# mLSTM features and router by products of small matrices, up-projections by high and low parts

## The chip, the cores and the metric

The kernel runs on one core of one Trainium2 chip. The metric is the device time of one execution in microseconds: the median of three runs. Five engines work side by side, each in the order of its own list: TensorE (PE: products and transposes), VectorE (DVE), ScalarE (ACT), GpSimd (POOL) and SyncE (SP), which issues nearly all transfers. They wait for each other by semaphores that are counted up.

## The reference

Two blocks run one after the other on 256 tokens of width 1024. The first has two layers of three kinds of attention and an MLP with 4096 hidden features. The second, which the change is about, does this (cut to what matters; `c` is a context of 256 tokens, `l` the 256 tokens of the result):

```python
q_lat, kv_lat, k_rope, xm, z, g_mla, g_ml = split(modulate(rmsnorm(x_or_ctx)) @ w_in)  # 384,256,64,1024 x4
q = rmsnorm(q_lat, q_norm) @ w_uq             # 8 heads of 192, only for l
k, v = split(rmsnorm(kv_lat, kv_norm) @ w_ukv)  # 8 heads of 128 + 128, for c and l
y_mla = softmax(q k^T) v
x_c = silu(conv5(xm))                          # along the tokens, each feature by itself
q, k, v = blockdiag4(x_c, w_qblk), blockdiag4(x_c, w_kblk), blockdiag4(xm, w_vblk)
gates = concat(q, k, v) @ w_gate + b_gate      # 16 numbers a token: input and forget, 2 directions, 4 heads
h = mlstm forward + mlstm backward             # decays from running sums and running maxima of the gates
y_ml = sigmoid(z) * (rms(h) * ml_norm + ml_skip * x_c)
x = x + g1 * ((sigmoid(g_mla) * y_mla + sigmoid(g_ml) * y_ml) @ w_out)
hm = modulate(rmsnorm(x, norm2), shift2, scale2)
aff = softmax(hm @ w_router)                   # 16 experts, each takes its 32 best tokens
x = x + g2 * (sum over experts of aff * ((silu(xs @ w_gate_e) * (xs @ w_up_e)) @ w_down_e))
out = rmsnorm(x)
```

The experts' weights are 16 x 3 matrices of 1024 x 1024 in fp32, 201 MB of the 395 MB that the kernel moves.

## The kernel before

**Weights.** Every weight comes as a unit of at most 128 x 4 x 512 numbers (1 MB). SP issues the loads in one fixed order, and each waits (`slots_free`) for the unit whose slot it takes. In the first block and in the input projection of the second, four slots are in turn (`R1 = 4`). There a product is made of two parts: ACT writes the high part of a unit (`split2_hi`, L569) into `ring_hi`, POOL writes the rest over the unit itself (`split2_lo`, L575), and `split_product` (L1726) makes three products in the fast format fp32r instead of one in fp32. From unit `U8 = U_UQ` on the eight slots of the ring (ring_lo and ring_hi together) are used as they are, and `product` (L1719) multiplies in fp32, which the profile lists as two instructions a product. Four units hold `w_uq` (128 x 3 x 384), four `w_ukv` (128 x 2 x 512), four `w_out`. The experts follow with 192 units in 16 slots: the ring and eight in the arena (`more_slots`). The first four expert units take slots that `w_ukv` leaves, units 4 to 7 wait for the four of `w_out`, and 8 to 15 stand behind them in SP's list.

**Order of the second block**, as PE has it (`tensor_block2`, L651): the ten input tiles (`input_tile`, L674), in between the turning of `xm` into features (`xm_features`, L678); the up-projections (`banks`, L652); transposes of queries and keys; 18 rounds of attention over 16 pairs of head and token tile (L785), in which round j makes scores j, turns the weights j-1 and multiplies by values j-2; then the features of the mLSTM. These are made in full: queries and keys for all 512 tokens (L816), the skip path's transposes (L825), value features (L831), gates from all of them (L843), value tokens (`values`, L849), two products that pick out the gate rows (L861). DVE then makes 14 dependent steps of gate arithmetic on 8 partitions (`step`, L1202), with an Exp and a Ln of ACT between the third and the fourth. After all 14 PE turns the rows (L867), and the four heads follow (L899): decay rows, raw scores, numerators. Their norm, gain, gate and sum are one piece at the end (L1281 to L1295). The output projection (L931), the addition to x (`add_gated`, L1299), the norm (L1971), the transposes and the modulation follow, the router's 32 instructions (L939), the softmax, four rounds of the eight largest (L1338) with their indices, the spread of indices over the partitions (L952, L955), the matrices that pick tokens (L1350, L1352) and put them back (L1356), the gather of the first four experts (L976), and the experts (L959).

**Around it.** ACT's list (L1463 to L1484) has the high parts between the copies and sigmoids; at L1466 it waits for DVE's sums of squares of the latents and takes a root, then come the high parts 9 and 10 and only then the sigmoid of tile 3, which PE waits for (`sig_sb` 1, L707) before tile 4. POOL makes the block-diagonal matrices after the last unit of `w_ukv` (L1636).

## Time and profile before

| | us |
|---|---|
| median of 3 runs (1775.72 to 1781.25) | 1776.74 |
| profiled execution, its own time | 1783.21 |
| span of the profiled execution | 1781.4 |
| TensorE busy, share of the span | 1542.3, 87% |
| VectorE, ScalarE, GpSimd busy | 486.0, 501.8, 579.9 |
| mean granted TensorE clock, share of full speed | 0.928 |

The span goes from the first to the last instruction. Starts are counted from its beginning. A row of a timeline gives start, duration, engine, line, operation, what is written and read, the number of instructions merged into the row, and in brackets the idle time before it with what ended it. A matmul's duration holds its way through the array, so consecutive ones overlap; their pace is the distance of their starts.

### The profile page before, as it was taken

How to read it: one execution, taken by the hardware profiler on the slowest of the kernel's cores; microseconds unless marked ns; L12 is line 12 of the kernel's file. 1: busy time of each engine (PE TensorE's matmuls, PEld its weight loads, DVE VectorE, ACT ScalarE, POOL GpSimd, SP SyncE). 2: the span in 40 equal slices, each digit the busy share in tenths (PEclk: the TensorE clock that was granted, in tenths of full speed). 3: DMA queues.
4: the chain of work that ended last, by engine and by line, in shares of the span. 5: the costliest groups of instructions: out<-in, count | busy, mean ns of one | idle time of the engine just before them, and what ended most of it. 6: DMA issues, size and time to landing. Idle time of an engine off the chain costs nothing. (4 is left out here: it accounts for less than half of the span.)

```text
span 1781.4 us, 17171 instructions
## 1 busy us (share of the span) xinstructions
PE 1542.3 (87%) x7300; PEld 1007.1 (57%) x7300; DVE 486.0 (27%) x802; ACT 501.8 (28%) x654; POOL 579.9 (33%) x158
## 2 busy tenths in 40 slices
PE   6999999999999999999989999786876676676665
PEld 5776688877867678877878755464443131131111
DVE  1223332421222233232451348444220000000001
ACT  4255343333435344343433124322110000000000
POOL 4655277545746277744375310000000000000000
PEclk9999999999999999999999999978878787888887
DMA  6534455696444255598244630000649999999995
GB/s 239 170 117 140 142 175 180 225 335 220 165 142 135 102 189 178 176 356 285 92 148 142 218 123 1 1 14 1 240 190 421 422 422 421 421 421 422 421 421 247
DMA packets 124920, 395.37 MB, mean 222 GB/s; under 512 B 6679, under 2 KB 10580, under 8 KB 100268
## 3 DMA queue, kind: packets, MB, share of 16 engines
q1 hardware_dynamic: 122960, 388.66, 58.5%
q0 software_dynamic: 1456, 4.51, 0.7%
q8 instruction: 58, 0.95, 0.2%
q10 hardware_dynamic: 428, 1.10, 0.2%
q14 instruction: 18, 0.15, 0.0%
HBM read 393.19 MB, written 1.05 MB: 221 GB/s over the span
## 5 line engine op out<-in xcount | busy, mean ns | idle before, releaser
L585 POOL TENSOR_TENSOR ring_lo<-ring,ring_hi 128x2048 fp32r<-128x2048 f32 x101 | 467.6, 4633 | 364.3 <-ACT ring_hi L566 364.3
L1730 PE MATMUL psum<-ring_hi,hT_lo 128*128 128x512 f32 (+2 forms) x880 | 354.3, 403 | 17.3 <-DVE hT_lo L1994 10.2
L1732 PE MATMUL psum<-ring_hi,hT_hi 128*128 128x512 f32 (+2 forms) x880 | 344.7, 392 | 0.0
L1731 PE MATMUL psum<-ring_lo,hT_hi 128*128 128x512 f32 (+2 forms) x880 | 342.9, 390 | 0.0
L566 ACT ACTIVATE ring_hi<-ring 128x2048 fp32r<-128x2048 f32 x116 | 222.0, 1915 | 384.2 <-DMA ring<-in_w_in 121.3
L968 PE MATMUL psum<-arena 128*32 128x512 f32 x768 | 133.2, 858 | 97.1 <-DMA arena<-in_w_e_up 36.1
L1730 PEld LDWEIGHTS psum<-ring_hi,hT_lo 128*128 128x128 f32 x880 | 166.8, 190 | 59.0 <-issue 13.8
L1732 PEld LDWEIGHTS psum<-ring_hi,hT_hi 128*128 128x128 f32 x880 | 166.6, 189 | 36.8
L1731 PEld LDWEIGHTS psum<-ring_lo,hT_hi 128*128 128x128 f32 x880 | 167.4, 190 | 32.9 <-issue 0.5
L968 PE MATMUL psum<-ring,arena 128*32 128x512 f32 x768 | 137.4, 705 | 43.2 <-DMA ring<-in_w_e_gate 17.5
L968 PEld LDWEIGHTS psum<-arena 128*32 128x32 f32 x768 | 30.8, 150 | 199.7 <-issue 81.3
L1722 PE MATMUL psum<-ring,arena 128*128 128x512 f32 (+1 forms) x272 | 113.0, 574 | 0.8 <-ACT arena L2337 0.8
L968 PEld LDWEIGHTS psum<-ring,arena 128*32 128x32 f32 x768 | 31.6, 124 | 141.0 <-issue 65.3
L578 POOL TENSOR_TENSOR ring_lo<-ring,ring_hi 128x2048 fp32r<-128x2048 f32 (+2 forms) x20 | 87.5, 4383 | 61.7 <-ACT ring_hi L573 61.7
L1730 PE MATMUL psum<-ring_hi,uT_lo 128*128 128x512 f32 x256 | 101.5, 396 | 0.0
L1732 PE MATMUL psum<-ring_hi,uT_hi 128*128 128x512 f32 x256 | 100.6, 393 | 0.0
L1731 PE MATMUL psum<-ring_lo,uT_hi 128*128 128x512 f32 x256 | 99.8, 390 | 0.0
L1722 PEld LDWEIGHTS psum<-ring,arena 128*128 128x128 f32 x272 | 51.3, 190 | 58.1 <-issue 50.2
L1585 ACT ACTIVATE arena<-psum 128x512 f32<-128x512 f32 x8 | 4.3, 594 | 239.7 <-PE psum L968 239.7
L585 DVE TENSOR_TENSOR ring_lo<-ring,ring_hi 128x2048 fp32r<-128x2048 f32 x15 | 38.7, 2578 | 100.5 <-ACT ring_hi L566 100.5
L1730 PEld LDWEIGHTS psum<-ring_hi,uT_lo 128*128 128x128 f32 x256 | 48.1, 188 | 13.8 <-issue 4.2
L1732 PEld LDWEIGHTS psum<-ring_hi,uT_hi 128*128 128x128 f32 x256 | 48.1, 188 | 10.6
(342 smaller groups left out, 1549.8 us busy)
## 6 DMA issues: line engine op xcount, KB each, us to landing
ring<-in_w_in SPq DMA_DIRECT2D x60, 1024.0 KB, 5.0
ring<-in_w_up SPq DMA_DIRECT2D x32, 1024.0 KB, 5.8
ring<-in_w_down SPq DMA_DIRECT2D x32, 1024.0 KB, 5.9
ring<-in_w_e_gate SPq DMA_DIRECT2D x32, 1024.0 KB, 26.7
arena<-in_w_e_gate SPq DMA_DIRECT2D x32, 1024.0 KB, 26.4
ring<-in_w_e_up SPq DMA_DIRECT2D x32, 1024.0 KB, 26.7
arena<-in_w_e_up SPq DMA_DIRECT2D x32, 1024.0 KB, 26.7
ring<-in_w_e_down SPq DMA_DIRECT2D x32, 1024.0 KB, 27.3
```

The lines of the kernel that those rows point to most:

```text
L566: act.activation(slot_hi(u), slot(u), ACT.Copy).then_inc(hi_sb, 1)
L578: pool.tensor_tensor(slot_lo(u)[:, :, 0:n], slot(u)[:, :, 0:n], slot_hi(u)[:, :, 0:n].bitcast(F32), ALU.subtract)\
L585: eng.tensor_tensor(slot_lo(u), slot(u), slot_hi(u).bitcast(F32), ALU.subtract).then_inc(done, 1)
L968: mm = pe.matmul(psum[32 * j:32 * j + 32, bank + n, :], lhsT[:, 2 * q + c, 32 * j:32 * j + 32], both[:, c * D + n * UN:c * D + (n + 1) * U ...
L1585: act.activation(hid[:, n, :], psum[:, n, :], ACT.Silu).then_inc(hid_a, 1)
L1722: last = pe.matmul(dst, lhsT(k0 + k), slot(u)[:, first + k, 0:n], start=start and k == 0, stop=stop and k == nk - 1)
L1730: pe.matmul(dst, lo(k0 + k), w_hi, start=start and k == 0, stop=False)
L1731: pe.matmul(dst, hi(k0 + k), w_lo, start=False, stop=False)
L1732: last = pe.matmul(dst, hi(k0 + k), w_hi, start=False, stop=stop and k == nk - 1)
```

## The change

The diff does this, part by part.

1. The units of `w_uq` and `w_ukv` go through the four slots too, with high and low parts (`SPLIT2`, `U8 = U_OUT`), and the latents get high and low parts (`qlT_hi`, `qlT_lo`, `kvlT_hi`, `kvlT_lo`; five more instructions on DVE). The units of `w_out` are reordered: upper halves of the rows first.
2. In ACT's list the sigmoid of tile 3 and the high parts 9 to 11 stand ahead of the root of the latents; a small Sigmoid is put before them. DVE's later work waits for `lat_root` 2.
3. Six rounds of the attention (2, 4, ..., 12) get a piece each on PE and a copy on ACT: the block matrices are turned, and from them and `w_gate` are made a map from features to gates (`gates_map`) and a map from features to scores (`scores_map`).
4. After the attention queries, keys and value features are not made. The gates are 16 products of `xm` and `xc` with `gate_map`; the scores take `xc` and `pF`, eight products of `qk_map` with `xc` (`mapped`).
5. The gate steps are reordered, add_skip is put between them, PE turns `af` and `ab` after step 9 and starts decay rows after step 12.
6. In the heads: numerators wait for the half of the previous head that they overwrite; `zg` gets the gain in advance; norm, gate and sum of heads 0 to 2 (`head_out`) stand ahead of head 3's readout.
7. The output projection begins with the upper four feature chunks; the branch is added in pieces.
8. The router multiplies x itself, not the normed x, by a weight with the modulation in it, in 8 products over four column groups, and scales its 16 sums afterwards; a row for the shift comes from `router_bias`. The top rounds have no index step; a running count gives each chosen token its place, and `pick` is made by comparing the place with the slot number. Group 0 of the experts begins when half of its features of each engine are copied; `pickT` is turned out of `weighed` later.

```diff
-U8 = U_UQ = U_IN + 2 * len(IN_TILES)
+U_UQ = U_IN + 2 * len(IN_TILES)
 U_UKV, U_OUT, U_EX = U_UQ + 4, U_UQ + 8, U_UQ + 12
+U8 = U_OUT
+SPLIT2 = [(4, IN_TILES[i // 2][1]) for i in range(2 * len(IN_TILES))] + 4 * [(3, 384)] + 4 * [(2, UN)]
...
+            src += [chunks(wout[UN * kh:UN * kh + UN, UN * n:UN * n + UN]) for kh in range(2) for n in range(2)]
...
+                load_expert(U_EX + i, expert_unit(i), unit_done(U_OUT + (i >= R + 5) if R <= i < RE else U_EX + i - (R if i < R else RE)))
...
+            def banks(outs, hi, lo, u, n, kc):
+                unit_ready(u)
+                for b, t in outs:
+                    last = split_product(psum[:, b, 0:n], tokens(hi, t), lo(t), 0, u, nk=kc, n=n)
+                last.then_inc(slots_free, 1)
...
+            def turn_block(i):
+                pe.wait_ge(bd_sb, i + 1)
+                for c in range(KC):
+                    last = pe.transpose(flat[3][:, c * P:(c + 1) * P], bd[i][:, c, :], ident)
+                last.then_inc(map_full, 1)
+            def gates_map(i):
+                pe.wait_ge(rows_in, 32)
+                for c in range(KC):
+                    if i == 0:
+                        pe.matmul(psum[:, 6, c * 16:(c + 1) * 16], turned_bd[0][:, c, :], wg[:, c, :], start=True, stop=False)
+                    last = pe.matmul(psum[:, 6, c * 16:(c + 1) * 16], turned_bd[1][:, c, :], wg[:, (1 + i) * KC + c, :],
+                                     start=i == 1, stop=True)
+                last.then_inc(map_full, 1)
+            def scores_map():
+                for c in range(KC):
+                    last = pe.matmul(flat[3][:, c * P:(c + 1) * P], turned_bd[0][:, c, :], turned_bd[1][:, c, :], start=True, stop=True)
+                last.then_inc(map_full, 1)
             NJ2 = H2 * TT
...
+                if j in MAP_ROUNDS:
+                    i = MAP_ROUNDS.index(j)
+                    if i:
+                        pe.wait_ge(map_sb, i)
+                    if i < 2:
+                        turn_block(i)
+                    elif i == 2:
+                        gates_map(0)
+                    elif i == 3:
+                        scores_map()
+                    elif i == 4:
+                        turn_block(2)
+                    else:
+                        gates_map(1)
                 if j < NJ2:
...
+            values(1)
+            pe.wait_ge(map_sb, 6)
+            for i in range(4):
+                if i >= 2:
+                    pe.wait_ge(xc_sb, 2 * i - 2)
+                for j in range(4):
+                    c = 4 * (i % 2) + j
+                    feat = xm[:, c, :, 2:2 + T] if i < 2 else xc[:, c, :, :]
+                    last = pe.matmul(psum[32 * j:32 * j + 32, 6, :], gate_map[:, 1 - i // 2, c, :], feat, start=i == 0, stop=i == 3)
+            last.then_inc(gp_full, 1)
+            pe.wait_ge(y2_sb, NJ2)
+            mapped(0, 2)
+            pe.wait_ge(gp_sb, 1)
+            pe.matmul(psum[0:8, 7, :], const("sel_i"), gp, start=True, stop=True)
+            pe.matmul(psum[0:8, 6, :], const("sel_f"), gp, start=True, stop=True).then_inc(gr_full, 1)
+            pe.wait_ge(vt_sb, 1)
+            mapped(1, 0)
+            pe.wait_ge(skip_sb, 2)
+            pe.wait_ge(vt_sb, 2)
+            turn_skip(0, 1)
+            pe.wait_ge(p_sb, 1)
+            turn_skip(1, 2)
+            pe.wait_ge(p_sb, 2)
+            values(2)
+            pe.wait_ge(sk_v, 2)
+            values(3)
+            pe.wait_ge(gr_v, 9)
             for d in range(2):
                 for t in range(4):
-                    pe.transpose(psum[:, 4, 32 * d + 8 * t:32 * d + 8 * t + 8], (af, ab)[d][:, t * P:(t + 1) * P], ident[0:8, 0:8])
...
+            pe.wait_ge(gr_v, 12)
+            pe.wait_ge(vt_a, 2)
...
+                else:
+                    pe.wait_ge(dec_a, 10 * MH)
+                    spread(1, 0)
+                if h == 0:
+                    pe.wait_ge(at_sb, 3)
+                    pe.wait_ge(sk_v, 4)
+                for t in range(TT):
+                    if h:
+                        pe.wait_ge(h_v, 8 * h - 2 + 2 * t)
...
+            pe.wait_ge(mix_v, 10)
+            turn_gated(0, 0)
+            pe.wait_ge(gb_sb, 1)
+            pe.wait_ge(turn_a, TURN_A + 9)
+            out_unit(0, 0)
+            pe.wait_ge(mix_v, 16)
+            turn_gated(1, 3)
+            out_unit(1, 0)
...
+            def head_out(h0, h1, mv, ready):
+                heads = slice(TT * h0, TT * h1)
+                dve.wait_ge(hn_a, ready)
+                dve.tensor_scalar(hst[:, 1, heads], hst[:, 0, heads], 1.0 / MD, EPS, ALU.mult, ALU.add).then_inc(mix_v, 1)
+                dve.wait_ge(hn_a, ready + 1)
+                dve.reciprocal(hst[:, 3, heads], hst[:, 2, heads]).then_inc(mix_v, 1)
+                dve.wait_ge(mix_v, mv + 2)
+                dve.wait_ge(zg_sb, 4)
+                for h in range(h0, h1):
+                    for t in range(TT):
+                        v = h_tok[:, t, h * MD:(h + 1) * MD]
+                        dve.scalar_tensor_tensor(out=v, in0=v, scalar=hst[:, 3, 2 * h + t:2 * h + t + 1],
+                                                 in1=zg[:, t, h * MD:(h + 1) * MD], op0=ALU.mult, op1=ALU.mult).then_inc(mix_v, 1)
+                mv += 2 + TT * (h1 - h0)
+                cs = slice(MD * h0, MD * h1)
+                for t in range(TT):
+                    dve.wait_ge(mix_v, mv)
+                    dve.tensor_tensor(gated[:, t, cs], gated[:, t, cs], h_tok[:, t, cs], ALU.add).then_inc(mix_v, 1)
...
+            router_bias()
+            out_unit(0, 1)
+            out_unit(1, 1)
+            pe.wait_ge(rt_v, 1)
             for t in range(TT):
+                pe.wait_ge(x2_v, 4 + 2 * t)
                 for k in range(KC):
-                    last = pe.matmul(psum[:, 0, t * NE:(t + 1) * NE], hT[:, k, t * P:(t + 1) * P], wr[:, k, :],
-                                     start=k == 0, stop=k == KC - 1)
+                    last = pe.transpose(flat[(0, 3)[k // 4]][:, k % 4 * T + t * P:k % 4 * T + (t + 1) * P], eighths(x[:, t, :], k), ident)
+                    if t == 1 and k % 4 == 3:
...
+                    pe.wait_ge(turn_a, TURN_A + 10)
+                for j in range(4):
+                    k = 4 * half + j
+                    last = pe.matmul(psum[32 * j:32 * j + 32, 0, 0:T], wr[:, k, :], hT[:, k, :], start=half == 0, stop=half == 1)
...
+                                if g == 0 and part == 0 and c == 0 and n == 0 and j == 0:
+                                    pe.wait_ge((xs_v, xs_a)[q // 2], 2 + 2 * (q % 2))
...
+            def add_branch(n, ts, first):
+                cs = slice(n * UN, (n + 1) * UN)
+                g = g_row1[:, cs].unsqueeze(1).to_broadcast([P, TT, UN])
+                dve.tensor_tensor(x_tmp[:, ts, :], DB[1 + n][:, ts, :], g[:, ts, :], ALU.mult).then_inc(x2_v, 1)
+                dve.wait_ge(x2_v, first + 1)
+                dve.tensor_tensor(x[:, ts, cs], x[:, ts, cs], x_tmp[:, ts, :], ALU.add).then_inc(x2_v, 1)
+            dve.wait_ge(slots_free, unit_done(U_OUT + 2))
+            add_branch(0, slice(0, 2), 0)
+            dve.wait_ge(x2_v, 2)
+            dve.wait_ge(o2_half, 1)
+            add_branch(1, slice(0, 1), 2)
+            dve.wait_ge(slots_free, unit_done(U_OUT + 3))
+            add_branch(1, slice(1, 2), 4)
+            dve.wait_ge(turn_full, FULL + 7)
+            dve.tensor_copy(hT[:, 0:4, :], flat[0].rearrange("p (k t) -> p k t", k=4)).then_inc(turn_v, 1)
+            dve.wait_ge(norm_a, NORM_A + 4)
...
+            dve.tensor_copy(part_sums, psum[:, 0, 0:T]).then_inc(rt_v, 1)
+            dve.wait_ge(norm_v, NORM_V + 3)
+            dve.wait_ge(rt_v, 1)
+            dve.wait_ge(lg_full, 2)
+            for t in range(TT):
+                dve.scalar_tensor_tensor(out=aff[:, t, :], in0=psum[:, 1, t * NE:(t + 1) * NE], scalar=r_sq[:, t:t + 1], in1=router_row,
+                                         op0=ALU.mult, op1=ALU.add).then_inc(rt_v, 1)
+            dve.wait_ge(rt_v, 5)
+            dve.tensor_reduce(rst[:, 0, :], aff, AX_X, ALU.max, negate=True).then_inc(rt_v, 1)
...
+            for half in range(2):
+                for t in range(TT):
+                    act.wait_ge(x2_v, 2 if half == 0 else 4 + 2 * t)
+                    act.activation(xn[:, t, half * UN:(half + 1) * UN], x[:, t, half * UN:(half + 1) * UN], ACT.Square,
+                                   accum_out=sums2[:, t, half:half + 1]).then_inc(norm_a, 1)
+            act.wait_ge(turn_full, FULL + 8)
             act.activation(hT[:, 4:8, :], flat[3].rearrange("p (k t) -> p k t", k=4), ACT.Copy).then_inc(turn_a, 1)
-            act.wait_ge(x2_v, 4)
-            norm(x, xn)
-            act.wait_ge(mod_sb, 4)
-            turn_modulated(FULL + 8, hT, lambda k: amp2[:, k:k + 1], lambda k: shift2[:, k:k + 1])
-            act.wait_ge(rt_v, 1)
+            act.wait_ge(norm_v, NORM_V + 2)
+            act.activation(half_r, means2, ACT.Sqrt).then_inc(norm_a, 1)
...
+            top_step(dve.tensor_scalar(chosen, affT, 0.0, None, ALU.is_lt))
+            top_step(dve.tensor_tensor_scan(out=count, data0=chosen, data1=chosen, initial=0.0, op0=ALU.add, op1=ALU.max))
+            top_step(dve.tensor_tensor(place, chosen, count, ALU.mult))
...
+            act.activation(table_ahead, amp1[:, 0, 0:1], ACT.Sigmoid).then_inc(lat_root, 1)
+            sigmoid(3, zg[:, :, 0:UN], 2)
+            high_parts(9, 11)
             act.wait_ge(lat_sq, 6)
             act.activation(lat[:, 2, :], lat[:, 1, :], ACT.Sqrt).then_inc(lat_root, 1)
-            high_parts(9, 10)
-            sigmoid(3, zg[:, :, 0:UN], 2)
-            high_parts(11, 12)
+            high_parts(12, 12)
             xm_half(1)
...
-            high_parts(19, 19)
+            high_parts(19, 20)
             sigmoid(8, gated[:, :, 0:UN], 2)
+            high_parts(21, 22)
             sigmoid(9, gated[:, :, UN:D], 0)
+            high_parts(23, 27)
             for n in range(4):
...
```

## Rows read from the trace of the kernel before

**Rows 1.** Stretches: from:to, length, busy PE PEld DVE ACT POOL (instructions), clock, DMA share, GB/s.
```profile
1058.00:1113.30 55.30, 54.90 (x256) 30.08 (x256) 46.63 (x103) 21.56 (x49) 0.00 (x0) 1.00 0.00 1
1113.30:1170.60 57.30, 40.72 (x193) 22.80 (x193) 28.11 (x32) 17.50 (x20) 5.53 (x6) 0.86 0.03 10
...
1272.00:1316.70 44.70, 27.89 (x105) 23.38 (x104) 19.89 (x53) 7.87 (x18) 0.54 (x1) 0.62 0.55 224
1320.40:1763.40 443.00, 298.20 (x1627) 90.86 (x1616) 20.44 (x32) 14.44 (x26) 0.00 (x0) 0.83 1.00 417
```

**Rows 2.** The chain of waits around the output projection: start, us, what.
```profile
1242.14 29.91 PE psum L1722 x64
1272.07 1.23 DVE arena L1306
```

**Rows 3.** Timeline of SP's queue: loads of expert units.
```profile
1320.40 5.22 SPq L642 DMA_DIRECT2D ring<-in_w_e_up  x8
```

**Rows 4.** The timeline of ACT and PE at the latents' root.
```profile
917.98 0.21 ACT L1467 ACTIVATE consts<-consts 128x6 f32<-128x6 f32 x1 [8.38 <-DVE consts L1043]
...
921.80 1.28 ACT L1461 ACT_TABLE_LOAD   x1
923.10 1.02 ACT L1461 ACTIVATE arena<-psum 128x1024 f32<-128x1024 f32 x1
...
924.22 0.76 PE L1730 MATMUL psum<-ring_hi,hT_lo 128*128 128x512 f32 x1 [4.58 <-issue]
```

**Rows 5.** The timeline at a 384-column split product and in the up-projections.
```profile
906.22 0.34 PE L1730 MATMUL psum<-ring_hi,hT_lo 128*128 128x384 f32 x1
906.39 0.34 PE L1731 MATMUL psum<-ring_lo,hT_hi 128*128 128x384 f32 x1
...
889.93 3.52 POOL L578 TENSOR_TENSOR ring_lo<-ring,ring_hi 128x1536 fp32r<-128x1536 f32 x1 [13.88 <-ACT ring_hi L573]
...
1014.74 0.96 DVE L1099 COPY arena<-psum 128x768 f32<-128x768 f32 x1 [2.91 <-PE psum L1722]
...
1036.21 0.60 ACT L1489 ACTIVATE arena<-psum 128x512 f32<-128x512 f32 x1 [5.78 <-PE psum L1722]
...
1043.08 0.69 DVE L1105 COPY arena<-psum 128x512 f32<-128x512 f32 x1 [5.51 <-PE psum L1722]
```

**Rows 6.** The timeline of DVE beside POOL's last subtraction and after it.
```profile
992.41 4.60 DVE L1094 TENSOR_TENSOR arena<-xn 128x128 f32<-128x128 f32 x1
...
997.07 0.28 DVE L1094 TENSOR_TENSOR arena<-xn 128x128 f32<-128x128 f32 x1
```

**Rows 7.** The timeline of PE: transposes, gate products, router products.
```profile
1052.80 3.66 PE L779 MATMUL psum<-consts,arena 128*128 128x128 f32 x32
...
1138.38 5.34 PE L845 MATMUL psum<-arena 128*16 128x512 f32 x48 [1.21 <-ACT arena L1526]
...
1283.78 6.98 PE L941 MATMUL psum<-consts,hT 128*128 128x16 f32 x32 [2.13 <-issue]
```

**Rows 8.** The timeline of DVE and PE around the gate steps.
```profile
1153.59 0.68 DVE L1212 SCALAR_TENSOR_TENSOR xn<-xn 8x512 f32<-8x512 f32 x1 [2.71 <-ACT xn L1530]
...
1161.20 0.41 DVE L1228 TENSOR_TENSOR xn<-xn,hT 8x256 f32<-8x256 f32 x1
...
1170.61 2.04 PE L884 MATMUL psum<-hT,consts 8*128 8x256 f32 x4 [2.02 <-ACT consts L1536]
```

**Rows 9.** The timeline at the last head and its gain.
```profile
1217.34 6.30 PE L912 MATMUL psum<-arena 128*128 128x257 f32 x28 [2.91 <-DVE arena L1278]
...
1229.28 3.26 DVE L1290 SCALAR_TENSOR_TENSOR arena<-arena,consts 128x256 f32<-128x256 f32 x8
```

**Rows 10.** The timeline of DVE and PE before the experts.
```profile
1294.43 0.40 DVE L1342 MATCH_REPLACE8 consts<-consts 16x256 f32<-16x256 f32 x1
...
1277.97 3.68 PE L1769 MATMUL psum<-consts,xn 128*128 128x128 f32 x16 [5.94 <-DVE xn L1987]
...
1307.07 7.92 PE L979 MATMUL psum<-arena,xn 128*128 128x128 f32 x32 [0.84 <-DVE arena L1350]
```

494 lines of the change are left out of this document (237 added, 257 removed).

## The prediction

> **What bounds the kernel now.** I read the table of stretches first, then the chain of waits, then the timelines of each engine where the chain goes through it. While the experts run, the DMA share is 1.00 at 417 GB/s for 443 us [rows 1]: 176 units of 1.049 MB, 2.52 us each. Before it the DMA engines do almost nothing through the attention and the mLSTM (1 and 10 GB/s, [rows 1]), since the experts' slots hang on the output projection. So the kernel has two parts. The last one is bound by transfers and starts when the first expert units are used up: from SP's first issue of that kind at 1320.40 [rows 3] to the end of the span are 461.0 us, which nothing in the change touches. All before it is one chain of computation: PE in the attention (54.90 of 55.30 us busy), DVE, ACT and PE in turn in the features of the mLSTM (PE 40.72 of 57.30) and before the experts (27.89 of 44.70, clock 0.62) [rows 1]. Time saved there moves the last part forward one for one, as long as the transfers that can be issued early are done by then.
>
> **Part by part** (us, negative is saved). Each stage starts where PE ends the one before.
>
> *Order of ACT at the latents' root.* PE waits 4.58 before tile 4, until 924.22, for the sigmoid that ends at 924.12; that stood behind the root (917.98), two high parts and a table load [rows 4]. Tile 3 ends at about 917.7, so the sigmoid can end at 918.9 with its table loaded early, and PE goes on at about 919.7 after the transposes of `xm`. The row at 924.22 has 0.76 for a product that takes 0.39 at full clock: eleven starts lie 0.43 apart instead of 0.23, 2.2 lost after the wait. High part 9 ends at 920.8 and its subtraction (4.6) at 925.4, needed at 930.7 as tile 4 has four token tiles; the root comes at 926, and the copies after it are needed at 941. Sum: -4.5 - 2.2 = -6.7. If the clock falls anyway, -4.5; if a high part is late, 0.
>
> *Up-projections.* A unit of `w_uq` takes PE 0.96 + 2.91 = 3.87 now, one of `w_ukv` 1043.08 - 1036.21 = 6.87, which is 16 instructions of 0.43 [rows 5]. By parts a product of 384 columns starts every 0.17 [rows 5], one of 512 every 0.23: 18 x 0.173 = 3.1 and 24 x 0.229 = 5.5. Sum: 4 x (3.1 - 3.87) + 4 x (5.5 - 6.87) = -8.5. The splitting must hide: POOL takes 3.52 for 1536 numbers [rows 5], so 2.6 for 1152 and 2.3 for 1024; with ACT's 1.1 and a load of 4.0 (576 KB) one unit is ready 7.8 after its slot is free, and three units of PE last 9.3. For `w_ukv` it is 7.5 against 16. The tightest is the last unit of `w_uq`, with 1.3 to spare. If the load took 6.9 us, as those of `w_ukv` do when four are issued at once, up to four units would be late by 1.6 each: +6. Range -9 to -2.
>
> DVE has five more instructions and its two-input ones run beside POOL. The row shows 4.60 for 128 x 128 numbers beside a subtraction and 0.28 after it [rows 6]. The rotation of the queries (4.1) starts at about 1026, when POOL has just made its last part; PE needs the copies behind it 4 us later. I take 0, at most +4.
>
> By the Trainium skill (SBUF — State Buffer, on the shared port pair) a VectorE operation with two SBUF inputs and a GpSimd operation exclude each other for a whole instruction. The 4.60 agrees with that, as it is the length of POOL's subtraction. By that rule each of DVE's two-input operations between the new splits may wait up to 2.6, and the sum would be nearer to the +4.
>
> *Maps in the attention.* 24 transposes at 3.66/32 = 0.114 [rows 7] are 2.7; `gates_map` has 24 products of 16 columns, 48 instructions. With 6.98/32 = 0.218 at half clock [rows 7], 0.11 at full clock (PEclk is 1.00 in the attention): 5.3. `scores_map` is 16 instructions of 0.128: 2.1. PE is the bound there, so all of it counts: +10.1. ACT's copies (1.02, from 128 x 1024 as in [rows 4]) lie after an exp whose successors PE asks for in the next round, about 0.5 in time. If they come late in the four rounds: +3. The ends are +8 and +16.
>
> *From the attention to the first decay row.* Now 1170.61 - 1113.3 = 57.3 [rows 8]. After, counted from the attention's end: two `values` 4.1; gates 32 instructions at 5.34/48 = 0.111 [rows 7], 3.6, to 7.7 (the last Silu ends at 4.0, no wait); `mapped` 1.7 while DVE copies; two selections 1.7, to 11.3. DVE Ff and |Ff| to 12.8. ACT has a copy that waits for the second `mapped` (13.0), to 14.1, then table load, Exp, table load, Ln (1.28, 0.63 each): 18.0. Behind `lf` step 12 ends 1161.20 - 1153.59 = 7.6 later [rows 8]: 25.7. PE has its skip transposes and values 2 and 3 done at 19, ACT its value copies at 21.7, so decay row 0 starts at 25.7. Sum: 25.7 - 57.3 = -31.6. add_skip(1) holds DVE to 29.1, and the first exps with it, but raw scores at half clock end at 34.2 either way, as now. Range -27 to -33; the upper end has each of some 20 handovers 0.2 later.
>
> *Heads and output projection.* Heads 0 to 2 are paced by PE at 10.8 each, unchanged. Head 3's numerators now start 2.91 late [rows 9]; the spread fills 1.9 of it and the finer wait frees them at 1216.4 instead of 1217.34. `head_out` of heads 0 to 2 needs g's copy, two squares, a table load and root, 6 x 0.41 (3.26/8, [rows 9]) and two sums of 0.95: done at 1225.1. PE turns it, ACT copies, and the first output unit starts at 1227.2 instead of 1242.14. The 64 instructions at 0.43 are 27.3 (29.9 now, with a slow start, [rows 2]), in them 8 transposes (0.9) and `router_bias` (1.8); head 3's own readout ends at 1231.4, under the first unit's 6.8. The last product ends at 1257.4 instead of 1272.07: -14.7 at full clock, -12 at the present pace. I take -13.5.
>
> *From the last output product to the first expert product.* Now 1316.78 - 1272.07 = 44.7 [rows 1, 2]. After: a quarter of the branch 1.4; 8 transposes at half clock (0.23) 1.8; copy 1.05; router half 1.3; copy of sums 0.4; summing 0.9; two small steps and the maximum 0.6, to 7.8 with handovers; ACT has two copies of x (2.1) and Exp's table load before it can do the exps, to 8.9; reciprocal and scaling 0.6; transposes and copy 1.1, to 10.6. Four rounds of 0.45 + 0.51 (MATCH_REPLACE8 0.40, [rows 10]), to 14.5; three steps 1.6; transposes 0.6; pick for group 0 0.6, to 17.3; gather 7.92 [rows 10]; two of four copies 0.8; start 0.2: 26.2. Sum: 26.2 - 44.7 = -18.5. What goes is the modulation, norm and half the router's products, 4 x 0.49 of index search, and the spread of indices (5.3 on PE, 2 on DVE). With full clock 20, with handovers of 0.2 more each 31: -13 to -24.7.
>
> The transfers bound this gain. After the last output product nine units are still to come, 22.7, and 2 to land; those and the first reuse of a slot (3.6 after the first expert product) give 24.7 against 29.8, so DMA idles 5 us and the computation still ends last. With the clock full, DMA would, and only 5.1 more could be had.
>
> By the Trainium skill (TensorE: Matmul & The Clock Gate, Part 4 on transposes) transposes don't count as work that gives PE its clock back. Today's 16 transposes at 1277.97 take 3.68 [rows 10], 0.23 each, at half clock after an idle stretch, and the router's products behind them run at 0.218 [rows 7], at half clock still. The rule would keep the half clock that I have taken up to the gather.
>
> **Sum.** -6.7 - 8.5 + 10.1 - 31.6 - 13.5 - 18.5 = -68.7. Against the profiled execution's own 1783.2 (span 1781.4 and 1.8 around it) that is 1714.5; it was 6.5 above the median of the runs, so for the median: 1776.7 - 68.7 = **1708**.
>
> **Rivals.**
> 1. *The attention loses its step.* Six rounds get a piece that waits for ACT's last copy, and PE's wait stops the round behind it. For: a round is 3.39 and PE has no gaps, so nothing absorbs a stall; against: two rounds lie between pieces. Each piece costs a whole round instead of its length: 6 x 3.39 = 20.3 instead of 10.1: 1718.
> 2. *Splits come late.* The units of the up-projections starve in four slots and the latents' reordering only moves the wait: +6 and +6.7: 1721. For: the tightest unit has 1.3; against: the input tiles run the same ring without a wait.
> 3. *Transfers end last before the experts.* Full clock to the gather, or fewer handovers: 5.1 less, 1703.
> 4. *Slower than before.* The transfers of the experts go slower into the new places or beside the new order. It decides from 2.52 to 2.91 us a unit (68.7/176 more), 417 to 361 GB/s: 1780 at 2.93. Against: 1.00 DMA share throughout, arena and ring alike, and the same sizes.
> 5. *It doesn't do what it says*: the new pieces sit on the chain unhidden and the old waits reappear as others, a third of the gain only: 1754. For: five long chains of handovers are reckoned, none measured.
>
> **Chances.** Forecast 0.60 (its own range 1702 to 1714), rival 1 0.13, rival 2 0.10, rival 3 0.12, rival 4 0.02, rival 5 0.03. The range 1700 to 1724 takes in the forecast and rivals 1 to 3. What this kernel's measurement can tell from no change is about 0.3%, 5 us: faster 0.97, same 0.01, slower 0.02.
>
> **What would show it.** Right: PE without the 4.6 us gap before tile 4; up-projections in 34.4 instead of 43; attention 65.4; 25.7 from it to the first decay row; 26.2 from the last output product to the first expert product with a short DMA gap; the experts' stretch 443 long at 417 GB/s. Wrong: waits of PE for `ring_lo` in the up-projections, for ACT's map copies in the attention, a first decay row later than 28, or an experts' stretch longer than 445.

## The result, and the profile after

| | before | changed |
|---|---|---|
| median, us (lowest to highest) | 1778.99 (1775.72 to 1786.34, 4 runs) | 1719.97 (1716.40 to 1722.94, 4 runs) |
| ratio, 95% interval | | 0.9662 (0.9624 to 0.9700) |
| profiled execution, its span | 1783.2, 1781.4 | 1722.94, 1721.2 |

The forecast was 1708 (1700 to 1724): direction and range were right, the centre was 12 us too low, and 1720 lies outside the forecast's own 1702 to 1714. The profiled execution of the changed kernel is the slowest of its four; a second one, taken later, spans 1712.2. Both are used below, because the difference between them is a lesson of its own.

First the table of stretches of the changed kernel, with the columns of [rows 1]: attention; from it to the first decay row; from there to the end of the output product; from there to the first expert product; the experts.

```profile
1046.90:1120.00 73.10, 72.80 (x346) 44.41 (x347) 46.90 (x103) 25.66 (x56) 0.32 (x1) 0.88 0.11 44
1120.00:1145.40 25.40, 19.40 (x141) 13.95 (x139) 15.42 (x19) 13.32 (x16) 5.70 (x6) 0.91 0.07 24
1145.40:1230.90 85.50, 81.38 (x298) 54.98 (x299) 39.14 (x86) 22.84 (x69) 0.00 (x0) 0.95 0.11 37
1230.90:1256.20 25.30, 15.72 (x78) 12.00 (x77) 12.17 (x36) 8.02 (x15) 0.00 (x0) 0.80 0.92 374
1259.80:1702.80 443.00, 288.22 (x1635) 89.24 (x1624) 21.68 (x33) 14.44 (x26) 0.55 (x1) 0.85 1.01 418
```

The last two stages and the one behind the attention stand as forecast; the experts are still one stretch of 443 us, now at 418 GB/s. The attention is the surprise: PE is busy for 72.80 of 73.10 us, so it waits for nothing, and yet the clock column is 0.88, where [rows 1] show 1.00. Stage by stage, from the starts and ends of PE's rows in three traces (us); between the up-projections and the attention lie 8.1 more (transposes of queries and keys and a wait of 1.41), equal in all three and in no line:

| stage | before | changed | changed, second trace | forecast of the change |
|---|---|---|---|---|
| start of input tile 4 | 924.2 | 924.0 | 918.0 | -4.5 |
| input tiles from there and up-projections | 125.5 | 114.8 | 114.8 | -2.2 - 8.5 |
| attention | 55.5 | 73.1 | 70.0 | +10.1 |
| to the first decay row | 57.3 | 25.4 | 25.4 | -31.6 |
| to the end of the output product | 101.4 | 85.5 | 85.7 | -13.5 |
| to the first expert product | 44.8 | 25.3 | 25.3 | -18.5 |
| experts, to the end | 464.6 | 465.0 | 464.9 | 0 |
| whole span | 1781.4 | 1721.2 | 1712.2 | -68.7 |

The first line holds the first block too, whose code is the same; the profiled executions of the changed kernel and of the variants below that keep its new order reach tile 4 at 918.0 to 924.7, so single spans differ by some 6 us by what lies ahead of tile 4, most of it code that was not changed. That is why the stages are compared, and medians only as far as they carry.

Next the timeline of the changed kernel on ACT and PE at the latents' root (as [rows 4]): the sigmoid's table is loaded early, the sigmoid ends at 923.55, and tile 4 starts at 923.99 with 0.48 and then at distances of 0.22 to 0.32, with no wait of 4.58 ahead. The root comes at 930.73.

```profile
914.34 1.28 ACT L1597 ACT_TABLE_LOAD   x1
...
922.53 1.02 ACT L1592 ACTIVATE arena<-psum 128x1024 f32<-128x1024 f32 x1 [6.69 <-PE psum L1889]
...
930.73 0.21 ACT L1601 ACTIVATE consts<-consts 128x6 f32<-128x6 f32 x1
```

```profile
923.99 0.48 PE L1887 MATMUL psum<-ring_hi,hT_lo 128*128 128x512 f32 x1
924.31 0.39 PE L1888 MATMUL psum<-ring_lo,hT_hi 128*128 128x512 f32 x1
924.53 0.40 PE L1889 MATMUL psum<-ring_hi,hT_hi 128*128 128x512 f32 x1
```

In the up-projections ACT's copies behind two units of `w_ukv` lie 5.49 apart (6.87 in [rows 5]), which is the 24 x 0.229 of the forecast:

```profile
1027.97 0.60 ACT L1623 ACTIVATE arena<-psum 128x512 f32<-128x512 f32 x1 [4.41 <-PE psum L1889]
...
1033.46 0.60 ACT L1623 ACTIVATE arena<-psum 128x512 f32<-128x512 f32 x1 [4.41 <-PE psum L1889]
```

The last view is PE's timeline in the attention, around `gates_map(0)`. Its products of 16 columns start 0.22 apart by twos until 1072.49, and from 1072.77 on 0.43 apart; the rows of the attention behind it, L838 and L839, take 2.05 and 2.07 instead of 1.1, until the one at 1082.92 takes 1.12 again. No row in this stretch has an idle time in brackets.

```profile
1072.27 0.38 PE L806 MATMUL psum<-arena,xn 128*128 128x16 f32 x2
1072.49 0.45 PE L807 MATMUL psum<-arena,xn 128*128 128x16 f32 x2
1072.77 0.59 PE L806 MATMUL psum<-arena,xn 128*128 128x16 f32 x2
1073.20 0.59 PE L807 MATMUL psum<-arena,xn 128*128 128x16 f32 x2
...
1074.48 2.05 PE L838 MATMUL psum<-arena,hT 128*128 128x512 f32 x2
1076.46 2.07 PE L839 MATMUL psum<-arena 64*128 64x512 f32 x2
...
1081.08 1.91 PE L838 MATMUL psum<-arena,hT 128*128 128x512 f32 x2
1082.92 1.12 PE L839 MATMUL psum<-arena 64*128 64x512 f32 x2
```

### The profile page after: what moved, and what is told of

The parts are those of the page before. It is cut to its first block, busy times and chain, and to the rows that moved or that the text cites. A ratio compares the mean times of both kernels' runs of the same rounds, so it can differ in the third digit from the quotient of the medians.

```text
span 1721.2 us, 17390 instructions
## 1 busy us (share of the span) xinstructions
PE 1505.5 (87%) x7392; PEld 1007.5 (59%) x7392; DVE 475.9 (28%) x794; ACT 517.1 (30%) x675; POOL 601.0 (35%) x167
## 4 chain that ended last, share of the span: by engine, by line
PE 73%; DMA 20%; DVE 2%; ACT 2%; SPq 1%; issue 1%; ACTq 0%; DVEq 0%
PE psum L1887 16%; PE psum L1889 15%; PE psum L1888 15%; PE psum L1879 6%; DMA arena<-in_w_e_gate 5%; PE psum L1052 5%; DMA arena<-in_w_e_up 3%; DMA arena<-in_w_e_down 3%; DMA ring<-in_w_e_down 3%; DMA ring<-in_w_e_gate 3%; DMA ring<-in_w_in 2%; PE psum L1063 1%; SPq L653 1%; PE psum L2118 1%; PE psum L839 1%; PE psum L968 1%
## 5 line engine op out<-in xcount | busy, mean ns | idle before, releaser
L1052 PE MATMUL psum<-ring,arena 128*32 128x512 f32 x768 | 125.1, 646 | 42.3 <-DMA ring<-in_w_e_gate 18.5
L590 POOL TENSOR_TENSOR ring_lo<-ring,ring_hi 128x2048 fp32r<-128x2048 f32 (+4 forms) x28 | 107.8, 3859 | 64.2 <-ACT ring_hi L585 64.1
L1879 PE MATMUL psum<-ring,arena 128*128 128x512 f32 x160 | 69.9, 593 | 0.8 <-ACT arena L2473 0.8
L585 ACT ACTIVATE ring_hi<-ring 128x2048 fp32r<-128x2048 f32 (+4 forms) x28 | 45.0, 1610 | 74.1 <-DMA ring<-in_w_in 53.4
```

What stands on the lines that cost most here:

```text
L585: act.activation(slot_hi(u)[:, 0:c, 0:n], slot(u)[:, 0:c, 0:n], ACT.Copy).then_inc(hi_sb, 1)
L590: pool.tensor_tensor(slot_lo(u)[:, 0:c, 0:n], slot(u)[:, 0:c, 0:n], slot_hi(u)[:, 0:c, 0:n].bitcast(F32), ALU.subtract)\
L1052: mm = pe.matmul(psum[32 * j:32 * j + 32, bank + n, :], lhsT[:, 2 * q + c, 32 * j:32 * j + 32], both[:, c * D + n * UN:c * D + (n + 1) * U ...
L1879: last = pe.matmul(dst, lhsT(k0 + k), slot(u)[:, first + k, 0:n], start=start and k == 0, stop=stop and k == nk - 1)
```

## The experiments

All are made from the changed kernel. Their ratios are to the kernel before, run beside them on the same chip (1780.55 for the changed kernel again, the old order of ACT, the plain up-projections and the 128 columns; 1778.88 for the added products with late and early transfers and the fewer rounds; 1783.53 for the other four).

**The changed kernel again.** No edit.

> The changed kernel once more, as the yardstick of this set. If the 60 us of its first runs hold, 0.966 of the kernel before. Theory A says that the first block, which the change does not touch, scatters by some 4 us from execution to execution, and the half clock after the 16-column products of the first gates map (from 1072.8 to 1082.9 in its first profile) comes back in every execution; the half clock in the first rounds of the attention (1049.1 to 1055.7) may or may not. Rival B says both stretches of half clock are chance: then this profile shows the attention in about 65 to 68 us instead of 73.1.

Measured: 1714.02 (1713.49 to 1722.04), ratio 0.9640 (0.9613 to 0.9667), the stages as in the table. The attention takes 70.0, 3.1 less than in the first trace, which had its first rounds at half clock as well (L838 2.08 at 1049.10). The half clock behind `gates_map(0)` came back, as theory A has it. Beside these runs of the kernel before the change is worth 66.5 us, beside the earlier ones 59.0, by the same program.

**The old order of ACT at the root** (only ACT's list is shown).

```
-            act.activation(table_ahead, amp1[:, 0, 0:1], ACT.Sigmoid)
-            sigmoid(3, zg[:, :, 0:UN], 2)
-            high_parts(9, 11)
             act.activation(lat[:, 2, :], lat[:, 1, :], ACT.Sqrt)
+            high_parts(9, 10)
+            sigmoid(3, zg[:, :, 0:UN], 2)
```

> Root of the latents ahead of high parts 9 and 10 and of the sigmoid of tile 3, as in the kernel before; the rest as changed. If that wait and the slow clock behind it were worth what was reckoned, 6.7 us slower than the changed kernel, PE with a gap of 4.6 us before tile 4. If the up-projections' splits only need the time that the old order lost (the wait moves), within 2 us of the changed kernel.

Measured: 1723.83 (1720.52 to 1725.44), ratio 0.9678 (0.9656 to 0.9701). By stages the wait of PE is back with 4.8 and the tile behind it takes 1.6 more, +6.4; all other stages are equal within 0.1 to those of the second trace. The term of the forecast holds.

**Up-projections by plain products**, from the eight slots as before (only the product is shown).

```
-                    last = split_product(psum[:, b, 0:n], tokens(hi, t), lo(t), 0, u, nk=kc, n=n)
+                    last = product(psum[:, b, 0:n], tokens(a, t), 0, u, nk=kc, n=n)
```

> The up-projections in fp32 from the eight slots, as in the kernel before; the rest as changed. By the pace of PE: 8.5 us slower than the changed kernel (43.0 instead of 34.5 for the eight units). If the split units cost something elsewhere (DVE beside POOL), less than 6 us slower.

Measured: 1721.33 (1720.08 to 1726.53), ratio 0.9672 (0.9647 to 0.9696). The stage takes 123.3 instead of 114.8, +8.5, the forecast's term to the tenth. The attention behind it took 68.2 here, 1.8 less than in the second trace, which fits the median, 7.3 above 1714.02. The clock falls in this trace too, but not inside `gates_map(0)`: its 32 instructions run from 1075.3 to 1078.8 at full clock, the fall comes 1.2 us behind them, with PE busy all the time, and the half clock lasts 6.8 us where it lasts 10.2 in the changed kernel:

```profile
1075.40:1078.80 3.40, 3.40 (x33) 3.40 (x32) 1.35 (x4) 0.81 (x3) 0.00 (x0) 1.00 0.02 5
1078.80:1080.00 1.20, 1.20 (x5) 0.44 (x5) 0.00 (x0) 0.00 (x0) 0.00 (x0) 1.00 0.00 0
1080.10:1086.80 6.70, 6.70 (x17) 3.55 (x17) 3.22 (x7) 1.43 (x4) 0.00 (x0) 0.50 0.00 0
```

**mLSTM and router alone.** Both edits above at once.

> The changed kernel with both smaller parts undone: the sigmoid behind the root again, and the up-projections as plain products. What is left is the mLSTM, the order of the output projection and the router. Theory A (the parts add up): before tile 4 and in the up-projections +6.5 + 8.5 = +15 to the changed kernel, 1727 to 1733, so 47 to 53 below the kernel before. Theory B (they share a cover: later starts hide each other's waits, or the splits of the input tiles take the place of the wait): +7 to +11, 1721 to 1725.

Measured: 1731.60 (1727.70 to 1732.54), ratio 0.9707 (0.9682 to 0.9732). By the ratios that is 0.67%, 12 us, over the changed kernel; by stages the wait is 4.8 and the stretch from tile 4 on 124.8, together +14.8, against 6.4 + 8.5 = 14.9 from the two kernels apart; 1.9 of it is hidden in the whole by the attention, 68.2 as with plain up-projections alone. The parts add up, and the mLSTM with the output product's order and the router carries the rest, some 52 us of 1783.5.

**The gates maps in 128 columns.** The 16 columns are repeated eight times, so each product writes 128; no result changes.

```
-    pe.matmul(psum[:, 6, c * 16:(c + 1) * 16], turned_bd[0][:, c, :], wg[:, c, :], ...)
+    pe.matmul(eight(c), turned_bd[0][:, c, :], wg[:, c, :].unsqueeze(1).to_broadcast([P, 8, 16]), ...)
```

> The products of both gates maps with their 16 columns eight times over, 128 columns, into eight times the width of PSUM, from which ACT copies the first 16; same number of instructions, nothing else changed. Theory A: the clock falls in the attention because of the 16-column products; with 128 columns it stays, the map costs some 0.5 us more by itself and 5 us less in clock, so 4 to 5 us faster than the changed kernel, with PE's round after the first gates map at 3.4 instead of 6.6. Rival B (the fall is chance or comes from the number of weight loads): no faster, and half clock after the map as before.

Measured: 1715.39 (1713.64 to 1719.73), ratio 0.9631 (0.9609 to 0.9652). The attention takes 65.2, 9.7 more than before the change, at a granted clock of 1.00 throughout. But the whole is no faster: from the first decay row to the end of the output product it takes 89.2 instead of 85.7. PE's timeline of this kernel there:

```profile
1139.96 6.29 PE L929 MATMUL psum<-arena 128*128 128x256 f32 x16
...
1148.56 5.41 PE L929 MATMUL psum<-arena 128*128 128x256 f32 x16 [1.00 <-DVE arena L1352]
...
1193.82 10.07 PE L1882 MATMUL psum<-ring,hT 128*128 128x512 f32 x16 [1.16 <-issue]
```

and the same three groups in the second trace of the changed kernel:

```profile
1138.36 5.73 PE L926 MATMUL psum<-arena 128*128 128x256 f32 x16
...
1146.39 3.72 PE L926 MATMUL psum<-arena 128*128 128x256 f32 x16 [1.00 <-DVE arena L1349]
...
1189.98 8.80 PE L1879 MATMUL psum<-ring,hT 128*128 128x512 f32 x16 [1.16 <-issue]
```

0.56 + 1.69 + 1.27 = 3.5: the same instructions behind the same waits, but more of them at half clock. In the second trace of the changed kernel the clock is back at 1142.4, some way before the first group ends, and stays up through the second. Here it is back at 1145.2, just before the first group ends, and falls a second time at 1148.6, as the wait of 1.00 us before the second group ends, until 1152.0:

```profile
1145.50:1148.50 3.00, 2.06 (x12) 1.23 (x10) 2.21 (x5) 0.24 (x2) 0.00 (x0) 1.00 0.01 3
1149.00:1152.00 3.00, 3.00 (x8) 2.38 (x8) 0.16 (x1) 2.80 (x9) 0.00 (x0) 0.50 0.00 0
```

So the attention is 4.9 us shorter and the stage behind the first decay row 3.5 longer than in that trace, and the forecast of 4 to 5 us for the whole was wrong.

**The gates maps in two halves.** Half of the products in one round and half in the next, still 16 columns wide (shown in part; the scores map and the third turning come later).

```
-MAP_ROUNDS = (2, 4, 6, 8, 10, 12)
+MAP_ROUNDS = (2, 4, 7, 9, 11, 14)
+                if j + 1 in (MAP_ROUNDS[2], MAP_ROUNDS[5]):
+                    i = MAP_ROUNDS.index(j + 1)
+                    pe.wait_ge(map_sb, i)
+                    gates_map(i // 5, 0)
...
```

> The changed kernel with each gates map (16-column products) done in two halves in neighbouring rounds of the attention, the scores map and the third turning moved one to two rounds later. Theory A (a longer run of 16-column products, 32 instructions in gates map 0, is what the clock falls in): with 16 at a time it stays at 2.4 GHz and the attention takes 65 to 66 us, as with the wide map (65.2), against 70.0. Theory B (it is the sum of short products and turnings over the attention, or the place in time): the clock falls all the same, 69 to 73. Whole time 1710 to 1716 by A, 1714 to 1720 by B.

Measured: 1717.23 (1713.39 to 1721.80), ratio 0.9638 (0.9613 to 0.9663). The attention is 65.2 here too, the clock 1.00 over all of it, by the same instructions:

```profile
1044.10:1109.30 65.20, 64.72 (x346) 40.17 (x347) 46.82 (x103) 25.71 (x56) 0.40 (x1) 1.00 0.13 49
1134.70:1151.00 16.30, 15.26 (x46) 11.55 (x47) 6.91 (x13) 6.73 (x22) 0.00 (x0) 0.66 0.00 1
```

The same 32 instructions, with a round of the attention between the two sixteens, leave the clock up. Of all 13 traces of the changed kernel and its variants, the six with a gapless run of 32 or more 16-column instructions have the clock fall inside the run or at most 1.3 us behind it; the seven without one have no fall there. The second row is the start of the decays, at 0.66: raw scores 6.42 and 5.41, the output product's first 16 instructions 10.14, and the stage 89.4. Theory A was right on the attention, and its whole time of 1710 to 1716 was wrong, because the stage behind it was as long as with the wide map.

**Every map twice.** Each of the six pieces is issued twice, `for c in list(range(KC)) + list(range(KC))`.

> The changed kernel with every product and turning of the six map pieces in the attention issued twice (the second overwrites the first with the same values). Theory A (a piece costs what its instructions take, the rest of the 14.5 to 17.6 that the attention grew by is a stretch at half clock): attention 70.0 + 10.1 = 80, up to 86 if the longer run of 16-column products holds the clock down longer; time 1724 to 1731. Theory B (a piece costs the round it sits in, by its handover with ScalarE, and its length hardly counts): attention 70 to 74, time 1714 to 1719.

Measured: 1735.85 (1730.93 to 1741.78), ratio 0.9734 (0.9708 to 0.9761), above the 1724 to 1731 of theory A; attention 86.3, 16.3 above 70.0 and just over theory A's upper end. Its stretches:

```profile
1047.00:1073.30 26.30, 26.17 (x148) 17.00 (x149) 16.79 (x35) 9.01 (x20) 0.34 (x1) 1.00 0.32 123
1073.30:1087.80 14.50, 14.50 (x46) 9.40 (x45) 3.22 (x7) 1.43 (x4) 0.00 (x0) 0.53 0.00 1
1087.80:1111.00 23.20, 23.20 (x150) 16.97 (x150) 14.50 (x32) 8.16 (x17) 0.00 (x0) 1.00 0.00 1
1111.00:1122.20 11.20, 11.20 (x30) 5.93 (x30) 3.23 (x7) 1.43 (x4) 0.00 (x0) 0.55 0.00 0
```

The clock now falls twice: in `gates_map(0)` and, as that too is 32 short products long here, in `gates_map(1)`. The half-clock stretches cost 14.5 x 0.47 + 11.2 x 0.45 = 11.9, against 10.2 x 0.50 = 5.1 in the changed kernel; the other 16.3 - 6.8 = 9.5 are the instructions themselves, as the wide map's 9.7. A piece costs its length, and no round is lost: rival 1 is refuted.

The stage from the first decay row to the end of the output product takes 88.8 here, with the second fall as in the wide map (second group of raw scores 5.30, first output products 10.01), although the clock had fallen twice in the attention. So a full clock in the attention is not what the longer stage needs, and nothing shows that the time won there causes it.

**Work in PE's waits.** The wide map, and 28 products of 256 columns into unused parts of PSUM before the waits at the gate steps, before the first heads are turned and in the router (one of the seven places is shown).

```
+            def fill(b, n):
+                for _ in range(n):
+                    pe.matmul(psum[:, b, T:2 * T], ident, modrow[:, 2, 0:T], start=True, stop=True)
             ...
+            fill(7, 3)
             pe.wait_ge(gr_v, 12)
```

> The kernel with the wide gates map, and 28 products of 256 columns into unused parts of PSUM put where TensorE waits (before the attention-side maps, before the first heads are turned, in the router), so that it is busy there. Theory A (what the changed kernel loses against the forecast is TensorE's clock: a stretch at 1.2 GHz in the attention, one at the start of the decays or of the output product, one in the gathering of the tokens): the attention stays at 65 us (70.0 in the second execution of the changed kernel), decays to the end of the output product fall from 89.2 to 84 to 86, the gathering from 7.9 to 4 to 5, and the time is 1706 to 1711, 5 to 9 below the wide map alone (1715.4). Theory B (the clock is not it; the chain through VectorE and ScalarE sets these stages): the stages stay at 85.7 to 89.2 and 25.3, the time at 1714 to 1718 or, with the added products in the way, up to 1722. Theory C (the transfers of the second eight expert tiles are last before the experts): the router's stage shortens by 3 to 4, but the experts' part grows by as much, 1711 to 1714.

Measured: 1714.42 (1709.87 to 1717.31), ratio 0.9626 (0.9603 to 0.9649). Decays to output product 85.8 instead of 89.2, as expected, and the output product's first 16 instructions 7.13 instead of 10.07, which is nearly all of it. The first raw scores are at full clock too, 3.72 instead of 6.29, but that brings nothing: the wait for VectorE behind them grows from 1.00 to 3.64, and the second ones take 5.88 at half clock. The gathering did not follow: 7.91, and the router's stage is 25.0, 0.2 shorter. The time is above the 1706 to 1711 of theory A, and 1.0 below the wide map's, which the scatter hides; the profiled execution had the attention's first rounds at half clock (68.2), as the first trace of the changed kernel.

**Earlier expert transfers.** The same, with SP's order `[0, 1, 2, 3, 4, 9, 10, 11, 12, 5, 13, 14, 15, 6, 8, 7]` for the first 16 tiles.

> The same kernel with the expert tiles 8 to 15 issued earlier: 9 to 12 right after the first product of the output projection, 13 to 15 after the second, 8 after the third, in place of all eight behind the last one. Theory A: no change against fill_late (within 2 us), since the queues run dry before the experts start in both (5.8 us without a transfer in the changed kernel, some 2 after 4 us of gain). Theory C: 3 to 4 us faster than fill_late. Rival D (transfers beside the output product slow its weights or VectorE): 1 to 3 us slower.

Measured: 1713.13 (1709.75 to 1715.80), ratio 0.9621 (0.9598 to 0.9644). The stages are equal to those of the kernel before this one within 0.1, but for the attention (65.2 against 68.2), and the experts' part is 465.6 in both. Moving the transfers brings nothing.

**Fewer rounds in the router, with late and with early transfers.** `for r in range(CAP // 8)` becomes `range(1)`.

> fill_late with one of the four rounds that find the eight largest scores; it leaves out the other three (some 2.8 us of VectorE's work ahead of the gathering) and so chooses fewer tokens. Theory A: the router's stage is 2.8 shorter than in fill_late; of that 1 to 2.8 reach the end, since the transfers (20 us for 8 tiles from the end of the output product on) now end after the experts' first tiles are free. Theory C: nothing reaches the end, time equal to fill_late within 1.

> cap_late (three of the four rounds left out) with the expert tiles 8 to 15 issued earlier. Theory A: 0 to 2 us below cap_late, 2.8 below fill_early. Theory C: 3 to 7 us below cap_late, 2.8 below fill_early.

Measured: 1709.17 (1706.53 to 1713.16), ratio 0.9597 (0.9574 to 0.9621), and 1711.27 (1706.23 to 1716.53), ratio 0.9611 (0.9586 to 0.9636). The router's stage takes 22.6 in both, 2.5 less than with four rounds, and the experts' part does not grow: 464.9 and 465.4, against 465.6. So by the stages all of it reaches the end; the medians are 5.3 and 1.9 lower, which cannot tell 2.5 from their scatter. The stretches of the one with late transfers:

```profile
1230.00:1244.00 14.00, 12.39 (x53) 10.25 (x51) 5.10 (x17) 3.33 (x7) 0.00 (x0) 1.00 1.02 427
1244.00:1246.00 2.00, 1.58 (x7) 1.39 (x6) 0.38 (x2) 0.38 (x2) 0.00 (x0) 1.00 0.99 414
1246.00:1248.00 2.00, 1.50 (x16) 0.65 (x20) 2.00 (x6) 1.98 (x5) 0.00 (x0) 1.00 0.92 377
1248.00:1250.00 2.00, 2.00 (x24) 0.70 (x20) 0.19 (x1) 0.43 (x1) 0.00 (x0) 1.00 0.04 16
```

The transfers run dry (0.04) before SP's next issue at 1250.12: 2.7 us less of computation than in the changed kernel leaves them hidden. In no run did the transfers come last before the experts, so rival 3 did not occur; its 5.1 us less of computation was never reached.

The gathering took 7.88 here at a clock of 1.00, and 7.93 in the changed kernel at 0.60. Both stretches, of the changed kernel and of the one with fewer rounds and late transfers:

```profile
1247.40:1255.20 7.80, 7.80 (x32) 7.69 (x32) 0.82 (x2) 0.00 (x0) 0.00 (x0) 0.60 0.97 405
```

```profile
1237.70:1245.50 7.80, 7.80 (x32) 7.69 (x32) 0.88 (x2) 0.00 (x0) 0.00 (x0) 1.00 1.01 422
```

The clock does not set the gathering. The weight loads (PEld) are busy for 7.69 of 7.80 in both, 336 and 334 ns each in the mean, where those of the scores map take 192 at a clock of 1.00; so the gathering seems bound by its loads. Why they are slow was not tried; their weights are every eighth number of a row.

**Work before the second raw scores too.** The kernel with added products and early transfers, without the products in the router, and

```
+                if h == 0:
+                    pe.wait_ge(sk_v, 4)
+                    fill(5, 12)
                 pe.wait_ge(w_v, 4 * h + 4)
```

> fill_early without the added products in the router, where the gathering took 7.9 at a granted clock of 0.67 and of 0.99 alike, and with 12 products of 256 columns in the wait before the second head's raw scores (3.6 us of TensorE's, after which those 16 products took 5.92 against 3.72). Theory A (the half clock follows that wait): raw scores 3.7 to 4.0, first decay row to the end of the output product 83 to 84.3 against 85.8, time 1708 to 1712. Theory B (the clock falls again at the next wait, or VectorE and ScalarE set the heads): 85.5 to 87, time 1712 to 1716.

Measured: 1713.82 (1710.50 to 1718.68), ratio 0.9619 (0.9596 to 0.9642). The timeline of PE:

```profile
1138.20 5.45 PE L882 MATMUL psum<-arena,consts 128*128 128x256 f32 x24
1143.48 3.62 PE L935 MATMUL psum<-arena 128*128 128x256 f32 x16
```

The raw scores are at full clock (3.62 against 5.92), 2.3 won, but a product of this type is two instructions, the 12 take 5.3 and the wait had 3.6: 1.7 is lost again, and the stage is 85.1 instead of 85.8, 0.6 less than in the second trace of the changed kernel. (The gathering's clock that the expectation names is that of longer stretches; in the gathering itself it is 0.60 in the changed kernel and 0.78 in the one with early transfers.) Whether eight of them would bring the 2.3 was not tried. None of the five variants that were to win time and leave nothing out (both edits of the gates maps and the three kernels with added products) can be told from the changed kernel by its time: their ratios and its own when run again, 0.9619 to 0.9640, lie in each other's intervals. What is said of them rests on the stages of one trace each.

## Why the prediction was right, and where it missed

- **ACT's order, -6.7.** Right: 4.8 of wait and 2.2 of slow clock behind it are gone (7.0 in the traces); undoing it gave +6.4 by stages.
- **Up-projections, -8.5.** Right: 125.5 - 114.8 - 2.2 = 8.5, and 8.5 by undoing them. The splits hid in four slots and PE shows no wait for `ring_lo`, so rival 2 fell. DVE's operations beside POOL did wait: L1198 takes 3.29 and the copy behind it 2.70, both while POOL subtracts, where L1198 takes 0.28 after it (the same in [rows 6]). But nothing of it reached PE, so the +4 did not come. The Trainium skill (SBUF — State Buffer, on the shared port pair) has a VectorE operation with two SBUF inputs and a GpSimd operation exclude each other; the 3.29 of L1198, which has two inputs, agrees with that.

```profile
991.22 3.29 DVE L1198 TENSOR_TENSOR arena<-xn 128x128 f32<-128x128 f32 x1
994.43 2.70 DVE L1199 COPY arena<-arena 128x128 f32<-128x128 f32 x1
```

- **Maps in the attention, +10.1: the step that failed.** The sum over instructions was right (9.7 where the clock stayed up), but it said "PEclk is 1.00 in the attention" and priced the new pieces at that clock, as if they could not change it. `gates_map(0)` brought 32 instructions in a row that write 16 columns each, the clock went to 1.2 GHz in them (or, with plain up-projections, 1.2 us behind them), with PE never idle, and the attention rounds behind them ran at double length. The attention grew by 14.5 in one trace and, with its first rounds at half clock as well, by 17.6 in the other; that other stretch is not explained. No rival had this. Rival 1 had the place right and the mechanism wrong: its 20.3 would have come from waits, and there were none. That its 1718 is the number nearest to the measured 1720 is chance.
- **To the first decay row, -31.6.** Right: 25.4 against 25.7. The chain through DVE sets it: work in PE's waits left it at 25.4.
- **Heads and output product, -13.5.** Measured -15.9 and -15.7. The wait before head 3's numerators is 0.19 instead of 2.91 [rows 9], as forecast:

```profile
1188.51 6.33 PE L968 MATMUL psum<-arena 128*128 128x257 f32 x28 [0.19 <-DVE arena L1402]
```

What was not forecast is that the output product starts 53.5 after the first decay row and not 56.6. 2.6 of these 3.1 lie before the first head's numerators, where the forecast had taken the present pace: the second raw scores ran at full clock, 3.72 instead of 5.41, and started 9.9 after the first decay row instead of 10.8, as more of the first ones ran at full clock. That is luck with the clock: in the kernels with the wide map, the halves and every map twice the second ones were back at 5.3 to 5.4. From its start to the last product the output projection takes 32.0, 1.8 more than forecast, all of it the slow start (8.80 for what takes 7.03).
- **To the first expert product, -18.5.** Right within 1: 25.3 against 26.2. The half clock that was forecast for the transposes did not occur; eight take 1.16, where 0.23 for each (1.8) was taken:

```profile
1232.43 1.16 PE L1013 MATMUL psum<-consts,x 128*128 128x128 f32 x8 [0.62 <-DVE x L1422]
```

PE comes out of the output product at full clock and waits only 0.62, where it had waited 5.94 [rows 10]. The rule of the Trainium skill cited there (TensorE: Matmul & The Clock Gate, Part 4, on transposes) was not put to a test, since there was no half clock to leave. Wrong was the lower end, "With full clock 20": it needs the gathering to get shorter with the clock, and that took 7.9 at 1.00 as at 0.60. With the clock at 1.00 all through and three of the four rounds left out, the stage still took 22.6.
- **Transfers.** From SP's reissue at 1259.82 to the end are 461.4, forecast 461.0; DMA ran dry for 5.8 before it. Rivals 3 and 4 fell. Rival 5 fell too: the gain is nearly the whole forecast, by stages, and not a third of it.
- **The sum.** By the second trace the stages give -69.2 and the forecast was -68.7: +4.4 in the attention is made up by -2.2 in the heads, -1.0 in the router, -0.3 before the decays and -1.7 in the first block. That these cancel is luck: the largest of them, in the heads, came from the clock, and the last is scatter. In the first trace the attention has 3.1 more and the first block, which is not part of the change, 6.0 more: -60.2. The medians gave -59.0 the first time and -66.5 the second. The forecast also took the 1776.7 of three runs as its base; larger samples of the kernel before gave 1778.9 to 1783.5, which is another 2 to 7 us.

## What to carry to other kernels

An instruction that is moved into a stage that runs at full clock is priced by its own length and by what it does to that clock: here a gapless run of 32 instructions of 16 columns cost 3 to 5 us on top of its own time, and splitting it over two rounds took that away. Then look at what the next stages do, because here the stage two further on took 3.5 us more at half clock in both repaired kernels, and its cause is open. A faster piece behind which another engine is waited for brings nothing: the raw scores at full clock gave their 2.6 us to the wait for VectorE. Compare stages and not totals when an unchanged block ahead scatters by more than the effect, and before pricing a stage by the clock, see whether its weight loads fill it.

## What the hardware showed unexpectedly

- The granted clock fell to half with PE busy throughout: inside a gapless run of 128x16 instructions (at 1072.7 and 1064.0 in two executions of the changed kernel, 1073.4 and 1110.9 with every map twice) or 1.2 us behind it, in products of 512 columns (1080.0 with plain up-projections). It stayed there for 6.8 to 13.7 us and came back with PE still busy. With 16 such instructions at a time, or with the same number writing 128 columns, it stayed at 1.00.
- The same program can show the attention's first rounds at half clock or not (73.1 and 70.0 of two executions). What decides it is not settled.
- Behind the same waits (3.9 and 1.7 us before the first decay row, 1.00 before the second raw scores) the clock fell once in five traces (stage to the end of the output product 85.5 to 85.7) and twice in three (88.8 to 89.4). The three are the wide map, the halves and every map twice, so it does not go by whether the attention before ran at full clock; what decides it was not settled.
- 32 instructions of 128x128 in fp32 with new weights each, in the gathering, take 7.9 us at a clock of 0.60 and of 1.00 alike, with PEld 99% busy.
